# One gather per block of a mixture of experts: token rows of 8 KB to 64 partitions, or half rows of 4 KB to 128 partitions

## What is computed

```
t = h.reshape(B * L, D)                      # D = 2048
gates = ...                                  # top-1 group, then top-2 experts in it
for e in range(N_EXPERTS):                   # 16
    he = silu(t @ w_exp_gate[e]) * (t @ w_exp_up[e])      # 2048 x 512 each
    out = out + gates[:, e:e + 1] * (he @ w_exp_down[e])  # 512 x 2048
```

## Time and profile before

| what | value |
|---|---|
| median of 3 runs (lowest, highest) | 1558.45 us (1552.96, 1559.66) |
| span of the profiled execution, from its first to its last instruction | 1555.7 us |
| PE busy | 1409.3 us, 91% of the span |
| DVE busy | 748.9 us, 48% |
| ACT busy | 241.6 us, 16% |
| POOL busy | 74.0 us, 5% |
| DMA | 422.20 MB, mean 271 GB/s |

### The profile page before, as it was taken

The page is one execution under the profiler, slowest core; times in us unless marked ns, Lnnn a source line. Parts: engine busy times, 40 slices in busy tenths (PEclk is TensorE's granted clock), DMA queues, the critical chain, the costliest instruction groups (busy, mean ns, idle before and its releaser), DMA issues.

```text
span 1555.7 us, 14305 instructions
## 1 busy us (share of the span) xinstructions
PE 1409.3 (91%) x5328; PEld 652.8 (42%) x5328; DVE 748.9 (48%) x1269; ACT 241.6 (16%) x401; POOL 74.0 (5%) x126
## 2 busy tenths in 40 slices
PE   2679999999999899999999999799899978999886
PEld 0135544444555455555544444533333333333332
DVE  0148888997775887968883723600000000000005
ACT  2101320100011111111211012511111110111014
POOL 3010000000010000000000000000000000000001
PEclk9889999999999999999999999899999988899899
DMA  9998457876669543221327734899999999999996
GB/s 347 428 371 264 144 181 258 275 241 220 201 200 321 173 143 97 80 88 63 134 69 293 232 112 163 310 395 404 411 375 388 405 400 396 398 389 381 405 425 276
DMA packets 132945, 422.20 MB, mean 271 GB/s; under 512 B 9897, under 2 KB 75668, under 8 KB 115032
## 3 DMA queue, kind: packets, MB, share of 16 engines
q1 hardware_dynamic: 120292, 375.79, 64.8%
q0 software_dynamic: 6496, 33.38, 6.3%
q10 hardware_dynamic: 6096, 12.20, 2.1%
HBM read 407.96 MB, written 22.58 MB: 277 GB/s over the span
## 4 chain that ended last, share of the span: by engine, by line
PE 70%; DMA 17%; DVE 8%; issue 3%; ACT 2%; ACTq 0%; POOL 0%; DVEq 0%; POOLq 0%; SPq 0%
PE ps L501 19%; PE ps L504 19%; PE ps L890 11%; DMA s_mem<-in_w_exp_gate 11%; PE ps L910 6%; DMA s_mem<-in_w_ada 3%; PE ps L775 3%; DVE s_mem L1767 2%; PE ps L672 1%; PE ps L448 1%; DMA s_mem<-in_hy_freq 1%; PE ps L623 1%; PE ps L430 1%; DMA y_slots<-s_mem 1%; DVE s_mem L1739 1%
## 5 line engine op out<-in xcount | busy, mean ns | idle before, releaser
L1593 DVE SCALAR_TENSOR_TENSOR s_mem<-s_mem,s_sT 128x512 f32<-128x512 f32 x480 | 339.4, 748 | 34.1 <-DMA s_mem<-in_w_ada 17.7
L501 PE MATMUL ps<-s_mem 128*128 128x384 f32 x1024 | 343.9, 493 | 1.1 <-DVE s_mem L1624 1.1
L504 PE MATMUL ps<-s_mem 128*128 128x512 f32 x672 | 292.8, 594 | 0.7 <-ACT s_mem L1364 0.7
L890 PE MATMUL ps<-s_mem 128*64 128x512 f32 x1152 | 263.5, 614 | 28.8 <-DMA s_mem<-in_w_exp_gate 27.6
L501 PEld LDWEIGHTS ps<-s_mem 128*128 128x128 f32 x1024 | 194.0, 192 | 143.4 <-issue 17.7
L504 PEld LDWEIGHTS ps<-s_mem 128*128 128x128 f32 x672 | 126.3, 190 | 158.5 <-issue 157.6
L890 PEld LDWEIGHTS ps<-s_mem 128*64 128x64 f32 x1152 | 91.1, 141 | 198.4 <-issue 198.4
L2059 DVE TENSOR_TENSOR s_mem<-s_mem,ps 64x512 f32<-64x512 f32 x18 | 12.2, 679 | 312.3 <-ACT s_mem L1462 312.3
L910 PE MATMUL ps<-s_mem 128*64 128x512 f32 x576 | 153.1, 693 | 9.3 <-DVE s_mem L2061 9.3
L910 PEld LDWEIGHTS ps<-s_mem 128*64 128x64 f32 x576 | 45.6, 157 | 103.5 <-issue 91.6
L2066 DVE COPY s_mem<-ps 128x512 f32<-128x512 f32 x18 | 12.4, 691 | 149.4 <-PE ps L910 149.4
(11 more groups left out here) (290 smaller groups left out, 1007.6 us busy)
## 6 DMA issues: line engine op xcount, KB each, us to landing
s_mem<-in_w_ada SPq DMA_DIRECT2D x256, 256.0 KB, 3.4
s_mem<-in_w_exp_gate SPq DMA_DIRECT2D x32, 2048.0 KB, 26.3
s_mem<-in_w_exp_up SPq DMA_DIRECT2D x32, 2048.0 KB, 31.2
s_mem<-in_w_exp_down SPq DMA_DIRECT2D x32, 2048.0 KB, 30.6
s_mem<-in_w_in SPq DMA_DIRECT2D x24, 2048.0 KB, 8.9
s_mem<-in_w_ada SPq DMA_DIRECT2D x16, 2048.0 KB, 11.9
s_mem<-in_w_out SPq DMA_DIRECT2D x8, 2048.0 KB, 8.2
y_slots<-s_mem ACTq DMA_DIRECT2D x34, 256.0 KB, 11.3
```

The lines of the kernel that those rows point to most:

```text
L501: m = mm(ps[:, banks[m_], 0:TOK], v[:, k, m_ * P:(m_ + 1) * P], hT[:, kk, :], start=(kk == 0), stop=(kk == KT - 1))
L504: m = mm(ps[:, banks[m_], :], hT[:, kk, m_ * P:(m_ + 1) * P], v[:, k, :], start=(kk == 0), stop=(kk == KT - 1))
L890: m = mm(ps[half, 0, :], hgT[:, kh * 8 + k, :], weights(e, 2 * kh + which)[:, k, :], start=(kh + k == 0), stop=(kh * 8 + k == KT - 1), ski ...
L1593: v.op(ve.scalar_tensor_tensor(out=o, in0=w, scalar=scale, in1=o, op0=ALU.mult, op1=ALU.add), S("piece_used") if last else None)
```

## The change

Every block is now gathered as the first one was laid down: 128 half rows of 4 KB on 128 partitions. `half_rows` is the same DRAM table seen as 768 rows of 1024 elements. The index table has 128 partitions, filled by twice as many small products, and the DVE copy of it becomes a multiply by 2 with the addition of 0 (partitions below 64) or 1 (`second_half`, a new constant column of `base`). An empty slot now gets 768 or 769, out of bounds as before. `turn_rows` becomes the first block's eight transposes of 128 x 128, and `turned` becomes the first block's copy. The buffer `hg` is 4 KB a partition where it was 8 KB.

```
-        idx_i = sb("idx_i", [BLK, MAXB + 1], I32)
-        idx_now = sb("idx_now", [BLK, 1], I32)
+        idx_i = sb("idx_i", [P, MAXB + 1], I32)
+        idx_now = sb("idx_now", [P, 1], I32)
...
-        hg = at(AT_MOD, D, rows=BLK)
-        first_x = at(AT_MOD, D // 2)
+        hg = at(AT_MOD, D // 2)
...
         h_dram = nc.dram_tensor("h_rows", [TOK, D], F32).ap()
+        half_rows = h_dram.rearrange("t (a n) -> (t a) n", a=2)
...
             def turn_rows():
                 for i in range(2):
-                    for q in range(8):
-                        m = tr(ps[:, 2 + i, q * BLK:(q + 1) * BLK], hg[:, i * (D // 2) + q:(i + 1) * (D // 2):8],
-                               ident[0:BLK, 0:BLK])
+                    for q in range(4):
+                        m = tr(ps[:, 2 + i, q * P:(q + 1) * P], hg[:, 4 * i + q:D // 2:8], ident[:, :])
                     m.then_inc(S("x_turns"), 1)
...
-            mm(ps[0:BLK, 7, 0:MAXB + 1], ones[:, 0:BLK], none_row, start=True, stop=False)
+            for a in range(2):
+                mm(ps[BLK * a:BLK * (a + 1), 7, 0:MAXB + 1], ones[:, 0:BLK], none_row, start=True, stop=False,
+                   skip_group_check=True)
             for i in range(2 * NT):
-                m = mm(ps[0:BLK, 7, 0:MAXB + 1], r_tok[:, i, :], r_blk[:, i, :], start=False, stop=(i == 2 * NT - 1))
+                for a in range(2):
+                    m = mm(ps[BLK * a:BLK * (a + 1), 7, 0:MAXB + 1], r_tok[:, i, :], r_blk[:, i, :], start=False,
+                           stop=(i == 2 * NT - 1), skip_group_check=True)
...
-                pool.indirect_dma_start(out=hg, out_offset=None, in_=h_dram,
+                pool.indirect_dma_start(out=hg, out_offset=None, in_=half_rows,
                                         in_offset=bass.IndirectOffsetOnAxis(ap=idx_now[:, :], axis=0),
-                                        bounds_check=TOK - 1, oob_is_err=False).then_inc(S("x_gathered"), 16)
+                                        bounds_check=2 * TOK - 1, oob_is_err=False).then_inc(S("x_gathered"), 16)
...
-                    A(hgT[:, 8 * i:8 * i + 8, :].rearrange("p k s -> p (k s)"), ps[:, 2 + i, :],
-                      ACT.Copy).then_inc(S("x_turned"), 1)
+                    A(hgT.rearrange("p (a k) s -> p k a s", a=2)[:, 4 * i:4 * i + 4],
+                      ps[:, 2 + i, :].rearrange("p (k a s) -> p k a s", k=4, a=2), ACT.Copy).then_inc(S("x_turned"), 1)
...
-            v.op(ve.tensor_copy(idx_i[:, :], ps[0:BLK, b, 0:MAXB + 1]), freed("dve", "index"))
+            v.op(ve.tensor_scalar(idx_i[:, :], ps[:, b, 0:MAXB + 1], 2.0, second_half, ALU.mult, ALU.add),
+                 freed("dve", "index"))
```

More of the change, by code:

```diff
@@ L76, in shape_constants @@
     tokens = np.arange(P)[:, None] + P * np.arange(NT)[None, :] - TOK
-    base = np.concatenate([ident, tri, sel.reshape(P, 2 * P), total, np.tile(rows, (P, 1)), tokens], 1).astype(np.float32)
+    lower = (np.arange(P) >= BLK)[:, None]
+    base = np.concatenate([ident, tri, sel.reshape(P, 2 * P), total, np.tile(rows, (P, 1)), tokens, lower], 1).astype(np.float32)
     masks = np.zeros((P, 2, P), np.int32)
@@ L153, in build @@
         gain = mem[:, AT_GAIN:MEM].rearrange("p (q n) -> p q n", q=4)
-        base = sb("base", [P, 4 * P + 32 + N_ROWS + NT])
+        base = sb("base", [P, 4 * P + 32 + N_ROWS + NT + 1])
         masks = sb("masks", [P, 2, P], I32)
@@ L178, in build @@
         tok_less = base[:, at_row + N_ROWS:at_row + N_ROWS + NT]
+        second_half = base[:, at_row + N_ROWS + NT:at_row + N_ROWS + NT + 1]
         ps = ctx.enter_context(nc.psum_tensor("ps", [P, 8, NCOL], F32))
@@ L852, in _ @@
             take(pe, 7, "index")
-            mm(ps[0:BLK, 7, 0:MAXB + 1], ones[:, 0:BLK], none_row, start=True, stop=False)
+            for a in range(2):
+                mm(ps[BLK * a:BLK * (a + 1), 7, 0:MAXB + 1], ones[:, 0:BLK], none_row, start=True, stop=False,
+                   skip_group_check=True)
             for i in range(2 * NT):
-                m = mm(ps[0:BLK, 7, 0:MAXB + 1], r_tok[:, i, :], r_blk[:, i, :], start=False, stop=(i == 2 * NT - 1))
+                for a in range(2):
+                    m = mm(ps[BLK * a:BLK * (a + 1), 7, 0:MAXB + 1], r_tok[:, i, :], r_blk[:, i, :], start=False,
+                           stop=(i == 2 * NT - 1), skip_group_check=True)
             m.then_inc(filled("index"), 1)
             pe.wait_ge(S("rows_kept"), 2)
[L858 to L861, removed]
+            turn_rows()
             pe.wait_ge(S("last_rows"), 1)
@@ L1438, in turned @@
                     act.wait_ge(S("x_turns"), value + i)
-                    A(hgT[:, 8 * i:8 * i + 8, :].rearrange("p k s -> p (k s)"), ps[:, 2 + i, :],
-                      ACT.Copy).then_inc(S("x_turned"), 1)
+                    A(hgT.rearrange("p (a k) s -> p k a s", a=2)[:, 4 * i:4 * i + 4],
+                      ps[:, 2 + i, :].rearrange("p (k a s) -> p k a s", k=4, a=2), ACT.Copy).then_inc(S("x_turned"), 1)
             for part in range(2):
                 act.wait_ge(S("rows_chosen"), part + 1)
-                a.op(A(first_x[:, part * NCOL:(part + 1) * NCOL], ps[:, 2 + part, :], ACT.Copy), S("rows_kept"))
+                a.op(A(hg[:, part * NCOL:(part + 1) * NCOL], ps[:, 2 + part, :], ACT.Copy), S("rows_kept"))
             act.wait_ge(S("tables_ready"), 1)
@@ L1451, in _ @@
             act.sem_inc(S("y_stored"), 1)
[L1452 to L1455, removed]
+            turned(2)
             b = read(act, "scatter")
```

## The result

The changed kernel takes 1530.72 us (median of 4 runs, 1526.96 to 1531.82), the kernel before 1559.06 beside it on the same chip. The ratio is 0.9822 (95% interval 0.98 to 0.9843): 28.3 us, or 1.8%, are gone. The profiled execution took 1530.56 us, with a span of 1528.7, which is 27.0 less than before.

What follows compares the result with a forecast made beforehand. The DMA queue, slowed by gathers onto partitions 0 to 63, was taken to bound the expert stage; 5.5, 10.8 and 6.7 us sum to 23.0, so 1558.45 - 23 = 1535 us, range 1525 to 1554.

Steps and rivals of the forecast that it cites:

- PE's waits: Expert stage: PE's waits for weights in the three parts would fall from 24.3 us to under 10.
- The three parts: Expert stage cut at 1160 and 1366 us; savings forecast as 5.5, 10.8 and 6.7 us, together 23.0.
- dry stretch: Queue ran empty at 1153 to 1162 and 1363 to 1369 us, at 279 and 310 GB/s; loss not counted as saving.
- the terms that I took off: Deducted from missing transfer time: dry queue 3.1, 0.8 and 0.8 us; gathers at 1145 and 1352 us, 1.7 and 2.5.
- the cap: Third part: 8.1 us saved, but only 7.1 winnable up to the last but one block's store; 6.7 taken.
- (a): Each block's transposes: 0.8 us shorter, worth nothing, since PE then waits 1.8 us for DVE's product.
- (b): PE's clock in down: emptier gap may drop it in four more blocks, 6.8 us at most; taken as 0.
- (c): Index table's seven more small products ahead of the first block's transposes: stage starts 0.9 us later; nothing at the end, 0.9 at most.
- (e): POOL issues the same number of DMAs with 128 indices in place of 64; it idles for most of a block: nothing.
- No change: Rival: scattered rows beside a full queue cost, not the partitions; 1557 to 1561 us, chance 0.12.
- The cost is per packet: Rival: 128 half rows cost twice what 64 rows do; 1582 us, chance 0.06.
- Half the gain: Rival: engines still get in each other's way, or the clock takes more; 8 to 16 us gained, 1543 to 1551, chance 0.12.

Runs made afterwards that it cites:

- 32 + 32 rows: Kernel before, 64 whole rows gathered onto partitions 0 to 31 and 64 to 95 with 128 indices, turned by 16 transposes of 128 x 128: 1530.6 us.

## Why the prediction was right

**The mechanism.** "I take it that the lower partitions' side of SBUF is the narrow place, and that the weights' packets for it wait and hold up their engines." Half of this is shown. The gathers did slow the whole queue, and it paid for them with PE's waits; the changed form takes this away, and with it 24.2 of the 28.3 us. The place of the rows is not the cause, as far as the part-filled blocks show. Either half by itself is slow, and 32 of 33 rows on partitions 0 to 31 pass at 427 GB/s once the DMA has 128 indices, where the kernel before had 283 with the same rows in that place. The step that went wrong is "What only the slow case has is a write of rows onto partitions 0 to 63": the slow gather was also the only one with 64 indices, while the one of the earlier trace rows has 128., on which "two queues at once don't do it" rests, is a weak case beside it, since 2.33 of its 2.54 MB are the token rows themselves. The change altered the place and the number of indices together, so it was luck that a forecast from the place came true. Had it moved the rows to the upper half only, the same reasoning would have promised a gain where the run shows none. Why the number of indices matters, and how packets wait inside, no run shows. The Trainium skill's rule in SBUF — State Buffer, "Door 1: The DMA port swizzle", gives partitions 0 to 63 half of the ports. The gathers with 64 indices, at 246 to 319 GB/s, agree with it on either half. By itself it doesn't tell why the 33 rows, of which 32 lie on partitions 0 to 31 in both runs, pass at 283 in one and at 427 in the other.

**The three parts.** SP's load that ends a dry stretch is the same instruction in both traces, and so is the first gather from `y_slots`. They stand at 1158.16, 1365.20 and 1516.27 us before, and at 1151.38, 1346.75 and 1489.30 after. The gain is 6.8, 18.5 and 27.0 us by then, which makes 6.8, 11.7 and 8.5 for the parts, forecast as 5.5, 10.8 and 6.7. The queue was the right place to count, and the terms that I took off were too large. Before anything was struck off for a gather that came too late for PE to profit, the missing transfer time was 7.3, 13.3 and 8.1 us, together 28.7; measured were 27.0. Of the two gathers struck off (1.7 and 2.5 us), 1.2 and 0.9 came back all the same. In the third part the cap fell as well; its 6.7 was in any case a choice under the 7.1 that had been worked out. I had ended it with the store of the last but one block, "issued at 1500 us after PE's work", as if only PE's work counted. The store is issued at 1470.36 now, 29.7 us earlier, and the end hangs on the last weights, which the queue brings earlier by itself. What is still missing in the three parts after is 140 x 7 / 425 + 194 x 4 / 425 + 144 x 3 / 425 = 5.1 us, where 33.4 had been, and the dry stretches alone (9 us each at 282 and 259 GB/s) account for it.

**PE's waits.** I expected under 10 us where 24.3 had been (27.6 with the wait before the last block); they are 18.7 (none in the first part, 11.6 and 7.1 in the others). This step failed too: I took it that what the queue gains comes out of the waits alone, and the 1.7 us a time for PE's clock behind a wait entered only into the third part. But PE gained as well, 8.9 us in down and 7.1 in gate and up, and the queue still sets the pace. The total of waiting and clock loss is what shrinks.

**(a) The transposes** at 1.16 us with a wait of 1.79 behind them are as forecast. Put back, they cost no more than the 1.7 us between the medians; "worth nothing" held in the kernel as it is. Without any gather, when the queue leaves PE more room, the whole of the other edits is worth 3.5.

**(b) The clock** went the other way. I feared that a gap with less work in it would make it fall in four more blocks. The down products show the count: all 576 at full clock are 127.6 us (18 times 7.09), and most blocks in which the clock falls take 1.7 more. In the timeline the kernel before has 14 blocks over 7.09 us (153.1 us in down), the changed one 10 (144.2). The Trainium skill's rule on idle gaps that spoke against the change (TensorE: Matmul & The Clock Gate, "HAM oscillation — how this bites in real kernels") agrees with one trace here: with the gap shortened by ACT's table load, the falls in down are gone. Gate and up then took 13.0 us more, behind longer waits for weights, and the granted clock of the whole profiled run hardly moved (0.967, and 0.965 with the table loads). Its consequence for this change, a loss of 6.8 us, did not come: the gap became emptier, but no longer. Why fewer blocks fell to the lower level, I can't say. Fewer and shorter waits for weights ahead of the gap would explain it, but turning twice (141.1 us in down) and 32 + 32 rows (146.2) had other counts with the same time, and no run tells these apart. The price of (b) is small either way, since 38.5 us of down and of the gap are worth 4.7.

**(c) The index table** costs nothing, not the 0.9 us that I gave it. Its 24 records, on the two halves of the columns, take 0.88 us where 12 took 0.86. They begin 1.0 us later than before (1009.49 against 1008.46), so the cause of that lies ahead of them, and no run shows it; counted from there, the stage gained 28.0 us and its first part 7.8:

```profile
1009.49 0.88 PE L859 MATMUL ps<-s_mem 128*64 128x28 f32 x24
1010.30 1.16 PE L834 MATMUL ps<-s_base,s_mem 128*128 128x128 f32 x8
```

**(e) POOL.** A gather of 128 indices takes POOL 1.01 us where one of 64 took 0.95; nothing waits for it.

**The rivals.** "No change", because scattered rows cost beside a full queue, falls with the 417 to 435 GB/s of the same rows in the changed form. "The cost is per packet" falls with the half rows on the lower partitions, at 1559.88 us. "Half the gain" lies outside of what was measured.

## What to carry to other kernels

When the DMA engines count as busy but move less than in an undisturbed stretch, look for a transfer that is issued for 64 partitions only, and issue it for 128, be it as half rows or as whole rows with indices out of bounds between them; judge it by what the other transfers lose, not by its own bytes. In this kernel the next thing to try is the smallest edit, which was not run: whole rows on partitions 0 to 63 as before, with 64 more indices out of bounds. And when two cases differ in speed, list everything in which they differ before naming the cause; here the place of the rows and the number of indices went together. Price PE's savings in a stage that the queue paces at what the waits leave of them: here 40.1 us of PE brought nothing before the queue was freed, and 38.5 brought 4.7 after. A one-column silu ahead of ACT's loop then gives the fastest version of the whole layer in this study, 1525.97 us.

## What the runs showed that I had not expected

- Gathers with 64 indices slow the queue on either half of the partitions (246 to 319 GB/s); gathers with 128 indices don't, not even with 32 of 33 rows on partitions 0 to 31 (427).
- A full product in float32 that turns a tile takes 7.87 us for 16, and 16 transposes of the same 128 x 128 take 2.04.
- Small products into both halves of PE's columns took 0.88 us for 24 records, where 12 into one half took 0.86.
- An activation ahead of the loop takes away 17 table loads of 1.28 us inside it, and with them the falls of PE's clock in down (127.6 us, its full-clock value), while gate and up become 13.0 us longer.
